# A four-layer float32 network on one core: half products of block two's attention grouped by four, output stored by tiles, another order at the head and at the FFN entry

## The reference, cut to what matters

```python
def conv_glu_ffn(h, ffn_w_in, ffn_conv_w, ffn_conv_b, ffn_w_out):   # first block
    u = causal_dwconv(h @ ffn_w_in, ffn_conv_w) + ffn_conv_b
    gate, up = jnp.split(u, 2, axis=-1)
    return (jax.nn.gelu(gate, approximate=True) * up) @ ffn_w_out
...
def second_block(...):
    for l in range(DEPTH):
        h = rms_norm_2(x, g_pre_mix[l])
        proj = h @ w_in[l]
...
        a_out = pool_mixer(u_pool, w_pool[l], pool_scale[l])
        b_out = dsa_attention(q, k, v, iq, ik, iw, topk)      # 8 heads of 64, the top 128 keys
        mix = jnp.concatenate([a_out, b_out], axis=-1) @ w_out[l]
        x = x + rms_norm_2(mix, g_post_mix[l])
        h = rms_norm_2(x, g_pre_ffn[l])
        f = jnp.square(jax.nn.relu(h @ w_ff1[l])) @ w_ff2[l]
        x = x + rms_norm_2(f, g_post_ffn[l])
    return x
```

## Time and profile before

| | before |
|---|---|
| median of 3 runs (lowest to highest) | 2762.08 us (2759.68 to 2762.48) |
| the profiled execution | 2765.85 us |
| its span | 2764.1 us |
| PE busy | 2685.1 us (97%) |
| ACT, DVE, POOL busy | 1102.5, 1098.6, 1211.5 us |
| DMA, mean rate | 79 GB/s |

### The profile page before, as it was taken

The page is one execution under the profiler, slowest core; times in us unless marked ns, Lnnn a source line. Parts: engine busy times, 40 slices in busy tenths (PEclk is TensorE's granted clock), DMA queues, the critical chain, the costliest instruction groups (busy, mean ns, idle before and its releaser), DMA issues.

```text
span 2764.1 us, 42821 instructions
## 1 busy us (share of the span) xinstructions
PE 2685.1 (97%) x15208; PEld 2112.3 (76%) x15208; DVE 1098.6 (40%) x2260; ACT 1102.5 (40%) x1871; POOL 1211.5 (44%) x630
## 2 busy tenths in 40 slices
PE   9999999999999999999999999999999999999997
PEld 7767777888877677788887666788888666788886
DVE  4455454441154553644402586510113586510112
ACT  4454254443345533544434235532333235532331
POOL 3323235555433232355544452464653452364653
PEclk9999999999999999999999999999999999999998
DMA  3211023333322100233232221133332221133332
GB/s 136 77 54 40 9 77 91 99 93 105 106 71 69 54 25 24 78 97 96 94 106 92 71 69 47 62 99 99 92 98 84 71 69 47 61 97 94 99 93 97
DMA packets 62867, 217.16 MB, mean 79 GB/s; under 512 B 6576, under 2 KB 6704, under 8 KB 62480
## 3 DMA queue, kind: packets, MB, share of 16 engines
q1 hardware_dynamic: 62416, 214.28, 24.7%
q0 software_dynamic: 320, 1.12, 0.2%
HBM read 213.28 MB, written 2.10 MB: 78 GB/s over the span
## 4 chain that ended last, share of the span: by engine, by line
PE 87%; DVE 5%; ACT 2%; issue 2%; DVEq 2%; POOL 1%; DMA 0%; ACTq 0%; SPq 0%; POOLq 0%
PE bank L1961 61%; PE bank L2337 3%; PE bank L2011 3%; PE bank L2190 2%; PE bank L2191 2%; PE bank L2192 2%; PE bank L2023 1%; PE bank L2222 1%; PE bank L2234 1%; PE bank L2245 1%; PE bank L2127 1%; PE bank L1995 1%; PE bank L2356 1%; DVE mT L1786 1%; PE bank L1988 1%
## 5 line engine op out<-in xcount | busy, mean ns | idle before, releaser
L788 POOL TENSOR_TENSOR wL<-raw,wH 128x1024 fp32r<-128x1024 f32 x371 | 893.1, 2408 | 1085.5 <-ACT wH L977 1085.4
L1961 PE MATMUL bank<-hH,wH 128*128 128x512 f32 x1680 | 679.8, 405 | 7.0 <-DVE mT L1786 4.2
L1961 PE MATMUL bank<-hL,wH 128*128 128x512 f32 x1680 | 657.9, 392 | 0.0
L1961 PE MATMUL bank<-hH,wL 128*128 128x512 f32 x1680 | 657.5, 391 | 0.0
L977 ACT ACTIVATE wH<-raw 128x1024 fp32r<-128x1024 f32 x371 | 392.2, 1057 | 531.1 <-PE bank L1961 490.8
L1961 PEld LDWEIGHTS bank<-hH,wH 128*128 128x128 f32 x1680 | 317.1, 189 | 102.4 <-issue 28.8
L1961 PEld LDWEIGHTS bank<-hH,wL 128*128 128x128 f32 x1680 | 317.3, 189 | 67.5 <-issue 6.0
L1961 PEld LDWEIGHTS bank<-hL,wH 128*128 128x128 f32 x1680 | 316.9, 189 | 67.8
L1961 PE MATMUL bank<-hidH,wH 128*128 128x512 f32 x864 | 336.7, 390 | 0.0
L1961 PE MATMUL bank<-hidH,wL 128*128 128x512 f32 x864 | 336.2, 389 | 0.0
L1961 PE MATMUL bank<-hidL,wH 128*128 128x512 f32 x864 | 336.1, 389 | 0.0
(11 more groups left out here) (378 smaller groups left out, 3629.9 us busy)
## 6 DMA issues: line engine op xcount, KB each, us to landing
raw<-w_dram SPq DMA_DIRECT2D x398, 512.0 KB, 3.5
x<-x_dram SPq DMA_DIRECT2D x4, 512.0 KB, 9.6
out_dram<-x SPq DMA_DIRECT2D x1, 2048.0 KB, 6.3
const<-const_dram SPq DMA_DIRECT2D x1, 1229.0 KB, 13.2
par_next<-par_dram POOLq DMA_DIRECT2D x5, 168.0 KB, 3.5
qkT<-pos_dram POOLq DMA_DIRECT2D x1, 256.0 KB, 7.3
const<-const_dram SPq DMA_DIRECT2D x1, 131.0 KB, 2.2
```

The lines of the kernel that those rows point to most:

```text
L788: pool.tensor_tensor(wL[:, s, :], raw[:, s, :], wH[:, s, :].bitcast(F32), ALU.subtract).then_inc(w_lo.sem, 1)
L1961: mm = pe.matmul((out or ACC[bk])[:, :], wt[:, c:c + P], rhs, start=first and k == 0 and j == 0, stop=last and k == tiles - 1 and j == 2)
```

## The change

Five edits. The attention's table gives four half steps to every fourth step in place of two to every second. The output goes out in eight DMAs, each when its tile of x is ready. At the head SP loads units 2 and 3 before the large part of the constants, ACT makes all eight hH tiles before the squares, PE does the third unit's high steps ahead of the norm's sums and its low steps with the others', and DVE takes the reciprocal after all eight hL. At the FFN entry the first two hidden pairs treat both halves together: scale both banks, shift both, then go on.

```diff
@@ FILL
-    _k = min(4 * KD - _f, (2, 0)[_n % 2])
+    _k = min(4 * KD - _f, (4, 0, 0, 0)[_n % 4])
@@ SP, head
+            for s in range(2):
+                load(Where(0, 0), d["w0"][2 + s], 1, s)
             sp.dma_start(const[:, CONST_FIRST:CONST_W], d["const"][:, CONST_FIRST:CONST_W]).then_inc(const_rest, 16)
...
-                with sp.Fori(1 - L, 14) as i:
+                with sp.Fori(2 * (1 - L), 14) as i:
@@ SP, end
-            sp.wait_ge(x_ready.sem, x_ready.at(Where(1, LAYERS), 0))
-            sp.dma_start(d["out"], x[:, :, :]).then_inc(stored, 16)
-            sp.wait_ge(stored, 16)
+            for k in range(KD):
+                sp.wait_ge(x_ready.sem, x_ready.at(Where(1, LAYERS), k + 1 - KD))
+                sp.dma_start(d["out"][:, k, :], x[:, k, :]).then_inc(stored, 16)
+            sp.wait_ge(stored, 16 * KD)
@@ ACT, norm
-                    act.activation(MT[w.b][:, k, :], x[:, k, :], ACT.Square).then_inc(sq_ready.sem, 1)
+                    if not first:
+                        act.activation(MT[w.b][:, k, :], x[:, k, :], ACT.Square).then_inc(sq_ready.sem, 1)
                 if first:
                     third_high(w, half)
+                    for k in range(KD):
+                        act.activation(MT[w.b][:, k, :], x[:, k, :], ACT.Square).then_inc(sq_ready.sem, 1)
                 fourth_high(w, half)
@@ ACT, hidden_pair
+                        if s == 0 or not late:
+                            shifted(s)
+                        if s == 0 and late:
+                            shifted(1)
                         for s_, more in units if late else ():
                             if s_ == s:
                                 next_high(w, i2 + more, s)
...
-                hidden_pair(0, 1, (THIRD, FOURTH), (), ahead=True)
+                hidden_pair(0, 1, (THIRD, FOURTH), (), late=True, ahead=True)
@@ DVE, hidden_pair
+                        if s == 0 or not both:
+                            scaled(s)
+                        if s == 0 and both:
+                            scaled(1)
                         dve.wait_ge(glu_in.sem, glu_in.at(w, i * 4 + 2 * q + s + 1))
...
-                hidden_pair(0, 0)
-                hidden_pair(0, 1, (THIRD, FOURTH))
+                hidden_pair(0, 0, both=True)
+                hidden_pair(0, 1, (THIRD, FOURTH), both=True)
@@ DVE, head
-            lows(Where(0, 0), 0)
+            lows(Where(0, 0), 0, KD)
@@ PE, first_three
+                if late:
+                    pe.wait_ge(w_lo.sem, w_lo.at(w, 2 * i2 + 3))
+                    for k in range(KD):
+                        high_step(k, 2)
                 norm_parts(w, half)
                 for k in range(KD):
                     pe.wait_ge(h_low.sem, h_low.at(w, KD * half + k + 1))
-                    for u in range(2 if late else 3):
+                    for u in range(3):
                         low_step(k, u)
...
-                if late:
-                    pe.wait_ge(w_lo.sem, w_lo.at(w, 2 * i2 + 3))
-                    for k in range(KD):
-                        high_step(k, 2)
-                    for k in range(KD):
-                        low_step(k, 2)
```

More of the change, by code:

```diff
@@ L1282, in hidden_pair, with shifted @@
                     i2 = i * 2 + q + 18
+                    def shifted(s):
+                        act.wait_ge(acc_scaled.sem, acc_scaled.at(w, i * 4 + 2 * q + s + 13))
+                        act.activation(mT1[:, 2 * q + s, :], banks[s][:, :], ACT.Identity,
+                                       bias=prmd(w, "fbias", i * 4 + 2 * q + s),
+                                       scale=prmd(w, "fconv", i * 12 + 6 * q + 3 * s + 2)).then_inc(glu_in.sem, 1)
                     for s in range(2):
@@ L1427, in residual, with lows @@
                     lows(*after)
-            def lows(w, half):
-                for k in range(KD):
-                    if k == KD - 2:
+            def lows(w, half, root_at=KD - 2):
+                for k in range(KD + 1):
+                    if k == root_at:
                         dve.wait_ge(norm_root.sem, norm_root.at(w, half + 1))
                         dve.reciprocal(rtok[:, :], root[:, 0, 0:NT]).then_inc(norm_inv.sem, 1)
-                    low(w, half, k)
+                    if k < KD:
+                        low(w, half, k)
             def layer_after(w):
@@ L1775, in _, with hidden_pair, scaled @@
                 dve.wait_ge(rstd_ready.sem, rstd_ready.at(w, 2))
-                def hidden_pair(i, q, banks=ACC):
-                    for s in range(2):
-                        buf = mT1[:, 2 * q + s, :]
+                def hidden_pair(i, q, banks=ACC, both=False):
+                    def scaled(s):
                         dve.wait_ge(unit_done.sem, unit_done.at(w, i * 4 + 37 + 2 * q + s))
@@ L1783, in hidden_pair @@
                                           ALU.mult).then_inc(acc_scaled.sem, 1)
+                    for s in range(2):
+                        buf = mT1[:, 2 * q + s, :]
+                        if s == 0 or not both:
+                            scaled(s)
+                        if s == 0 and both:
+                            scaled(1)
                         dve.wait_ge(glu_in.sem, glu_in.at(w, i * 4 + 2 * q + s + 1))
```

## The result

| | before | after |
|---|---|---|
| median of 21 runs each (lowest to highest) | 2763.96 us (2758.30 to 2766.97) | 2770.18 us (2764.28 to 2776.29) |
| span of the profiled execution | 2764.1 us | 2771.0 us |
| ratio of the times | | 1.0024 (95% interval 1.0018 to 1.0031) |

The account below looks back on a forecast made before the run. PE, busy 97% of the span, bounds the kernel, so only its waits and clock count. FFN -7.8, attention +11.6, clock +0.5, end -3.8, head -1.0 sum to -0.5: median 2761.6 us, range 2754.5 to 2769.5.

Parts of the forecast that it names:

- The FFN entry: First block's FFN entry, twice: PE's 2.25 us wait before unit 42 and the low clock behind it go, together -7.8 us.
- The rival that the wait stays: FFN entry: ACT's piece conversion or unit 40's shift is over 0.9 late, PE waits again, 2769.4 us; chance 0.08.
- The end: Tail behind SP's last issue: only the last 256 KB tile remains to land, 2.5 us in place of 6.3, -3.8.
- the line through two rows: Tail: landing time of 256 KB drawn between the DMAs of 131 KB (2.2 us) and 2048 KB (6.3), giving 2.5.
- The head: Start of the kernel: ACT's hH tiles come in 5 us, not 9; the wait ending at 52.46 ends earlier, -1.0 us.
- The waits of the attention: Block two's attention, twice: regrouped fill uncovers PE's transposes, waits 10.5 us in place of 4.7, +5.8 a layer, +11.6.
- the first kind: Attention steps 6, 14, 22, 30: transposes wait on ACT's row of five things; 1.2, 1.5, 1.3, 1.0, together 5.0 us.
- the second kind: Attention steps 2, 3, 7, 10, 11, 19: DVE's second head starts later behind the fill; waits together 4.8 us.
- The clock in it: Block two's attention: new waits bring 1.3 low-clock stretches, +2.1 us, less one old stretch of 1.6; net +0.5.
- that one goes: Attention, layer two: the low stretch behind step 13's 1.62 us wait, costing 1.6 us, vanishes with that wait.
- Low clock in the attention: Rival: six or more low stretches at 1.6 us each make it slower by over 0.2%; seven give 2770.7; chance 0.12.
- the prediction's own tests: Wrong if attention takes below 70 or above 77 us a layer, or low clock stands behind most of its waits.

Follow-up runs that it names:

- the three profiles with the long waits open: Profiled executions of the changed kernel (2770.18 us), the kernel before with only the new table (2781.80), and the changed kernel with idle matmuls in its five short waits (2766.64).
- fitted: Changed kernel with one half step a step, but two in steps 8, 11, 12 and none in 10, 23, 24, 27: 2740.59 us, run again 2742.01.
- another kernel: Changed kernel with idle matmuls only in the five short attention waits (steps 2, 3, 7, 27, 32), six long ones open: 2766.64 us, ratio 1.0012 against before.

## Why the prediction was wrong

**The FFN entry** was right: -7.8 foretold, -7.7 measured alone, -4.0 and -4.0 between the same matmuls. So was its working: the second piece took 0.69 in place of 2.20 once POOL's split no longer lay under it. The Trainium skill (GPSIMD Engine Reference, section Specifications) has GpSimd and VectorE share SBUF interfaces; with 0.69 clear of POOL and 2.20 under it the trace agrees. (The first piece, which the new order brings partly under a split, took 1.41; nothing waited for it.) The rival that the wait stays did not come.

**The end** was right: -3.8 foretold, -4.2 in the traces, since the last 256 KB land in 2.1 and not 2.5. The Trainium skill (DMA: Bandwidth & Descriptors, section Anatomy of one DMA), whose formula was measured on DMAs that GpSimd issues, gave 4.2 for the gain; here that was nearer than the line through two rows, though its 6.8 and 2.6 are both 0.5 above the 6.3 and 2.1 of these DMAs of SP.

**The head** was nearly right in size: -1.0 foretold, -0.8 from PE's first product on in the mean of nine traces against four. No run has the head alone. The steps of its working came true beside that product (ACT's eight hH in 5.0, the wait of 0.3 for ACT's copy, DVE's multiply 0.9 earlier relative to it). But the text named 51.5 as the clock time of the wait's end, and it did not allow for the landing that starts the head, which moves by 1.2 between runs.

Together the parts without the regrouping were foretold at -7.8 - 3.8 - 1.0 = -12.6 and measured at -12.6. That the figures meet to 0.1 is luck, since the measured one is uncertain by 4.

**The waits of the attention** were right in place and nearly in size. Of the first kind 1.2, 1.5, 1.3 and 1.0 were foretold for steps 6, 14, 22 and 30, and the rows have 1.06, 1.47, 1.25 and 1.03. Of the second kind 0.7, 0.4, 1.4 and 1.9 for steps 2, 3, 11 and 19 stand against 0.79, 0.46, 1.38 and 1.87; step 13 lost its wait and step 32 kept 0.78 for 0.7. Mis-sized were two: step 7 at 0.3 has 0.63, and step 27, where the text said "nothing (no top-k round there)", has 0.65: at the widths there DVE's and ACT's chain was long enough without a round. The sum is 11.4 in place of 10.5, and +6.7 a layer in place of +5.8: +13.4 in place of +11.6. (The lower bound of the working is mis-added: 3.6 + 4.0 + 0.7 - 4.7 is 3.6, not 3.9. Nothing hangs on it.)

**The clock in it** is the step that failed. The text took 1.3 new stretches, +2.1, less the one that was to go, net +0.5, by the share of waits between 1.0 and 1.8 us elsewhere in the trace behind which the clock fell (2 of 18). The medians say 18.7 - 13.4 = 5.3, the mean clock 6.4, the profiled execution 8. What failed is the share. It took 1.0 to 1.8 us as one kind of wait and said one in nine; behind the long waits of the new table the clock fell in one of four (9 of 36), all of them behind 1.38 and more. The trace before had that difference too: 2 of its ten waits of 1.36 to 1.72, none of the eight shorter ones. Waits under 1.0 were not counted, but in both layers of the profiled execution after the first stretch followed the pair of 0.79 and 0.46. And "that one goes" was said of the stretch behind step 13, where one layer in two had been seen: what went was a chance of one, not one. The 18 waits also lie across 2760 us, while these lie eleven in 79; whether the closeness itself lowers the clock was not tested. With 13.4 for 11.6 and 5.3 for 0.5 the sum of the prediction becomes -0.5 + 1.8 + 4.8 = +6.1, against +6.2 measured. That it closes is no proof, since the 5.3 is what the medians leave over; with the 6.4 of the mean clock it is +7.2, and the medians are uncertain by about 2.

The rival *Low clock in the attention* had the mechanism and, with six or more stretches, the time: "Without any low stretch there the sum is -2.6; each costs 1.6". Six in the profiled execution give +7.0, and its span is 6.9 longer. That the two agree so well is luck: the attentions cost 1.3 more than in this sum, and the head, the tail and the FFN entries gave 1.3 more. It was given 0.12. Against it the text held that 16 of 18 such waits kept full clock; for it stood the Trainium skill (TensorE: Matmul & The Clock Gate, section A second HAM failure mode), which reports a clock that swings when PE idles briefly and often between groups of matmuls. The trace agrees, with three stretches at 0.50 in each attention, and none in either once the idles are filled with matmuls. By the prediction's own tests, attention above 77 us a layer was to show it wrong: it took 79.1 in the profile after, and of the 79.1 the waits alone explain 74.5.

**What stays open.** Behind which of the waits the clock falls, and why there, is not known; where the stretches lie is seen in few executions only (six, four and one in the three profiles with the long waits open). Filling only the long waits came out 2.7 us below filling all (1.1 by the ratios, with a clock 0.0006 higher), which is no more than their uncertainty. What the low stretch of 10.2 us at 1004 in the profiled execution after has to do with the change is not known either; the other traces have 3.4 or nothing there.

## What to carry to other kernels

Fill work for an engine that waits on a chain across engines is worth most when it is spread over the waits, each getting as much as its own chain is long; grouping it leaves some waits bare and covers others twice. With all else alike, the four tables gave 2770.2 (by four), 2751.4 (by two), 2744.7 (by one) and 2740.6 us (fitted), with the same instructions on each engine. When a change makes waits of 1 to 2 us more frequent on PE, price the clock beside the wait, the longer ones above all: here it was 40 to 50% on top (5.3 or 6.4 on 13.4), and a few idle matmuls into a free bank took it away without making the waits longer. A mean over several executions is the price of such a thing; one trace shows its mechanism, not its size.

## What was not expected of the hardware

The same wait, in the same code, brings the low clock in one layer and not in the other: 1.38 did in the first layer of the changed kernel and did not in the second; in another kernel 1.48 did and 1.88 did not. Two short waits close together, 0.79 and 0.46, did so in both layers of one profile and in none of four layers of two others.

Matmuls of 128 columns hold the clock as well as wide ones. In the attention whose waits were filled PE had only transposes, scores, products with v and idle matmuls between one fill and the next, and the windows show 1.00 in both layers. Matmuls of one column may not. Four of the eleven low stretches ahead of the tail in the trace before (at 1124.7, 1759.5, 2121.3 and 2384.2) had no wait over 0.3 us in the 15 us ahead of them, but each came right behind two rows of sums over tokens (128x1, line 1988), 16 matmuls of one column each in about 2 us. One of them, from PE's timeline and the windows view:

```profile
1757.19 1.05 PE L1988 MATMUL bank<-const,sq_sum 128*128 128x1 f32 x8
1758.21 1.05 PE L1988 MATMUL bank<-const,sq 128*128 128x1 f32 x8
...
1760.00:1765.00 5.00, 5.00 (x26) 4.50 (x25) 3.64 (x7) 2.91 (x5) 2.37 (x1) 0.70 0.36 108
```

That the sums are the cause is an inference from where the stretches lie; no run without them was made.

The first landing of the head moves by more than its edit is worth: PE's first product started between 11.9 and 13.1 us over thirteen traces, and in the four with the old head alone it moved by as much.
